# Norm boundaries of a two-layer diffusion trunk: affine step in halves, token tiles multiplied one by one, modulation blocks loaded from GpSimd's queue

## The reference, cut to what matters

```
h = rmsnorm(x, g_mix_pre) * (1 + scale1) + shift1
x = x + gate1 * rmsnorm(mixer(h), g_mix_post)
h = rmsnorm(x, g_ffn_pre) * (1 + scale2) + shift2
x = x + gate2 * rmsnorm(conv_ffn(h, ...), g_ffn_post)
```

## Time and profile before

| | us |
|---|---|
| median of 3 runs (1643.89 to 1649.33) | 1647.64 |
| the profiled execution | 1646.06 |
| its span in the trace | 1644.3 |
| PE busy | 1555.4 (95%) |
| DVE busy | 1087.6 (66%) |
| ACT busy | 700.5 (43%) |
| POOL busy | 117.2 (7%) |
| mean granted TensorE clock | 0.972 of full |

### The profile page before, as it was taken

How to read it: one execution, slowest core, us unless ns; L and a number is a source line. 1 busy time by engine, 2 the same in 40 slices (tenths; PEclk the granted TensorE clock), 3 DMA queues, 4 the chain that set the end, 5 groups by cost and what they waited for, 6 DMA issues and landing times.

```text
span 1644.3 us, 27983 instructions
## 1 busy us (share of the span) xinstructions
PE 1555.4 (95%) x10553; PEld 1414.5 (86%) x10553; DVE 1087.6 (66%) x2082; ACT 700.5 (43%) x1263; POOL 117.2 (7%) x128
## 2 busy tenths in 40 slices
PE   6799898989999999999989989989899999999997
PEld 2699687879998789998779988768799988999986
DVE  5598766888777867778884248872866641466544
ACT  6631666354443234443252237662644432344332
POOL 1250220000000000000010032410000000000000
PEclk8799899999999999999989989999999999999999
DMA  8234101613334763334642220102222222222222
GB/s 328 105 115 129 33 2 59 211 52 105 113 115 147 217 174 115 115 105 168 198 135 69 75 81 2 44 4 76 61 82 77 70 71 89 73 70 76 70 81 92
DMA packets 45953, 164.54 MB, mean 100 GB/s; under 512 B 5584, under 2 KB 6608, under 8 KB 45104
## 3 DMA queue, kind: packets, MB, share of 16 engines
q1 hardware_dynamic: 42336, 152.00, 28.5%
q0 software_dynamic: 2320, 10.54, 2.0%
q10 hardware_dynamic: 1216, 0.92, 0.2%
HBM read 159.87 MB, written 3.57 MB: 99 GB/s over the span
## 4 chain that ended last, share of the span: by engine, by line
PE 81%; DVE 7%; DMA 2%; issue 2%; ACT 1%; ACTq 0%; DVEq 0%; SPq 0%
PE ps L1842 22%; PE ps L1843 22%; PE ps L1943 13%; PE ps L1935 6%; PE ps L2100 4%; PE ps L2129 4%; PE ps L2042 3%; PE ps L2115 3%; DMA work<-in_wmodt 2%; DVE work L1081 1%; PE ps L1867 1%; PE ps L2034 1%; PE ps L2116 1%; PE ps L2134 1%; DVE product L1081 1%
## 5 line engine op out<-in xcount | busy, mean ns | idle before, releaser
L1842 PE MATMUL ps<-hh,whi 128*128 128x320 f32 x864 | 268.4, 311 | 7.7 <-DVE wlo L1067 3.8
L1842 PE MATMUL ps<-hh,wlo 128*128 128x320 f32 x864 | 267.7, 310 | 0.0
L1843 PE MATMUL ps<-hh,wlo 128*128 128x320 f32 x864 | 267.6, 310 | 0.0
L1842 PE MATMUL ps<-hl,whi 128*128 128x320 f32 x864 | 267.6, 310 | 0.0
L1843 PE MATMUL ps<-hl,whi 128*128 128x320 f32 x864 | 267.6, 310 | 0.0
L1843 PE MATMUL ps<-hh,whi 128*128 128x320 f32 x864 | 267.6, 310 | 0.0
L618 ACT ACTIVATE whi<-raw 128x1024 fp32r<-128x1024 f32 (+1 forms) x112 | 117.0, 1046 | 319.8 <-PE ps L1843 286.8
L612 ACT ACTIVATE whi<-raw 128x1024 fp32r<-128x1024 f32 (+1 forms) x70 | 72.1, 1033 | 264.3 <-PE ps L1943 173.6
L1943 PE MATMUL ps<-whi,ffh 128*128 128x512 f32 x440 | 171.9, 391 | 3.4 <-DVE wlo L1067 2.6
L1067 DVE TENSOR_TENSOR wlo<-raw,whi 128x1024 fp32r<-128x1024 f32 (+1 forms) x72 | 87.5, 1216 | 131.8 <-ACT whi L612 128.6
L1943 PE MATMUL ps<-wlo,ffh 128*128 128x512 f32 x440 | 171.3, 389 | 0.0
(11 more groups left out here) (226 smaller groups left out, 2897.8 us busy)
## 6 DMA issues: line engine op xcount, KB each, us to landing
raw<-in_w SPq DMA_DIRECT2D x174, 512.0 KB, 3.5
work<-in_wmodt SPq DMA_DIRECT2D x56, 512.0 KB, 3.6
ring<-in_wmodt SPq DMA_DIRECT2D x24, 512.0 KB, 4.3
work<-in_wmod SPq DMA_DIRECT2D x16, 512.0 KB, 6.8
grow<-gate_rows POOLq DMA_DIRECT2D x4, 1024.0 KB, 5.8
work<-in_rpb POOLq DMA_DIRECT2D x8, 448.0 KB, 4.5
x<-in_x SPq DMA_DIRECT2D x5, 512.0 KB, 7.9
out_x<-x SPq DMA_DIRECT2D x5, 512.0 KB, 2.6
```

Source lines behind the costliest of these rows:

```text
L1842: T.matmul(bankA[s], slot(w, s, k), h[:, k, 0:HT], start=st, stop=sp_)
L1843: last = T.matmul(bankB[s], slot(w, s, k), h[:, k, HT:NT], start=st, stop=sp_)
```

## The change

1. The affine step of a tile is split in two halves of four instructions with a wait and a count of their own. `SCALAR_AFFINES` and `VECTOR_AFFINES` say who does which half; `affine_done` waits for both. The halves of tiles 0, 1, 3 and 4 are shared between both engines; in `mix_boundary` ACT does both of tile 2, in `fout1_boundary` they are shared too.
2. The orders of both engines in both boundaries are rewritten.
3. `piece` multiplies one slot by one token tile: 24 matmuls of 128 columns. It waits for the low part of that tile and slot only. PE turns tiles 0, 1 and 2 and then alternates pieces and the remaining turns.
4. Blocks 24 to 79 are issued by POOL's queue, in order, each after its buffer's last block is summed. `spread_gate(1, 0, 3)` stands behind block 55. SP's queue no longer waits for them.

```diff
+SCALAR_AFFINES = {"mix": ((0, 1), (1, 0), (2, 0), (2, 1), (3, 1), (4, 0)),
+                  "fout1": ((0, 1), (1, 1), (1, 0), (2, 0), (3, 0), (4, 1))}
+VECTOR_AFFINES = {"mix": ((0, 0), (1, 1), (3, 0), (4, 1)),
+                  "fout1": ((0, 0), (2, 1), (3, 1), (4, 0))}
...
+        def affine_done(engine, b, t):
+            kind = NORMED[b][1]
+            for half in range(2):
+                if (t, half) in SCALAR_AFFINES[kind]:
+                    engine.wait_ge(s_afa, len(SCALAR_AFFINES[kind]) * b + SCALAR_AFFINES[kind].index((t, half)) + 1)
+                else:
+                    engine.wait_ge(s_afd, len(VECTOR_AFFINES[kind]) * b + VECTOR_AFFINES[kind].index((t, half)) + 1)
...  SP's queue
-                if u == 23:
-                    sp.wait_ge(s_tl, 5)
-                if u == 45:
-                    sp.wait_ge(s_ffl, FH + 1)
-                if u == 79:
-                    sp.wait_ge(s_ffl, 2 * FH + 1)
                 for m in LOAD_AFTER.get(u, ()):
-                    sp.wait_ge(s_mused, chunk_before(m) + 1)
-                    chunk_in(m, chunk_buffer(m), ring0 if m < 24 else ring1)
+                    if m < 24:
+                        sp.wait_ge(s_mused, chunk_before(m) + 1)
+                        chunk_in(m, chunk_buffer(m), ring0)
...  affine on ACT (on DVE alike)
-            def affine(b, t):
+            def affine(b, t, half):
-                if t == 2:
-                    act.wait_ge(s_tl, 5 * b + 1)
+                if t >= 2:
+                    act.wait_ge(s_tl, 5 * b + t - 1)
-                for k in range(KD):
+                for k in range(4 * half, 4 * half + 4):
...  mix_boundary on ACT, from square_x(b, 2) on, as it is now
                 square_x(b, 2)
+                deviation_x(b, 2)
+                hi(u)
+                affine(b, 0, 1)
+                hi(u + 1)
+                h_hi(b, 0)
+                affine(b, 1, 0)
+                square_x(b, 3)
                 square_y(b, 1, 4)
...  mix_boundary on DVE
                 update_x(b, 3)
+                inverse_x(b, 2)
                 norm_x(b, 1)
-                affine(b, 0)
+                affine(b, 0, 0)
+                affine(b, 1, 1)
+                norm_x(b, 2)
                 lo(u)
                 h_lo(b, 0)
-                inverse_x(b, 2)
                 lo(u + 1)
+                inverse_x(b, 3)
                 gate_mixed(b, 1, 4)
-                norm_x(b, 2)
-                inverse_x(b, 3)
                 norm_x(b, 3)
...  POOL
+            pool.wait_ge(s_tl, 5)
+            for m in range(24, 80):
+                pool.wait_ge(s_mused, chunk_before(m) + 1)
+                if m == 36:
+                    pool.wait_ge(s_ffl, FH + 1)
+                if m == 67:
+                    pool.wait_ge(s_ffl, 2 * FH + 1)
+                b = chunk_buffer(m)
+                pool.dma_start(ring1[b], a["wmodt"][m]).then_inc(s_mlate[b], 16)
+                if m == 55:
+                    pool.wait_ge(s_yf, 10)
+                    pool.wait_ge(s_coef, 8)
+                    spread_gate(1, 0, 3)
...  PE
-            def piece(u0, c0, c1, bank, f, start, final):
-
-                for s in range(2):
-                    for k in range(KD):
-                        for n, (w, h) in enumerate(((whi, hh), (whi, hl), (wlo, hh))):
-                            last = T.matmul(ps[:, 2 * s + bank, f:f + c1 - c0], slot(w, s, k), h[:, k, c0:c1], ...)
+            def piece(b, u0, s, t):
+                pe.wait_ge(s_lo, u0 + s + 1)
+                pe.wait_ge(s_tl, 5 * b + t + 1)
+                if t == 0 and s == 0:
+                    affine_done(pe, b, 1)
+                if t == 0 and s == 1:
+                    pe.wait_ge(s_yf, 10 * yi + 5 + 3)
+                if t == 2 and s == 1:
+                    pe.wait_ge(s_yf, 10 * yi + 10)
+                bank, f = (0, P * t) if t < 2 else (1, P * (t - 2))
+                for k in range(KD):
+                    for n, (w, h) in enumerate(((whi, hh), (whi, hl), (wlo, hh))):
+                        last = T.matmul(ps[:, 2 * s + bank, f:f + P], slot(w, s, k), h[:, k, tile(t)], ...)
+            def mix_boundary(b, u0):
+                turn(b, 0)
+                turn(b, 1)
+                turn(b, 2)
+                piece(b, u0, 0, 0)
+                piece(b, u0, 1, 0)
+                turn(b, 3)
+                piece(b, u0, 0, 1)
+                piece(b, u0, 1, 1)
+                piece(b, u0, 0, 2)
+                turn(b, 4)
+                piece(b, u0, 1, 2)
+                piece(b, u0, 0, 3)
+                piece(b, u0, 1, 3)
+                piece(b, u0, 0, 4)
+                piece(b, u0, 1, 4)
```

More of the change, by code:

```diff
@@ L151, in chunks_loaded, with late_chunks_loaded @@
     return early + sum(1 for i in range(12, m + 1) if chunk_buffer(i) == b)
+def late_chunks_loaded(m):
+    return sum(1 for i in range(24, m + 1) if chunk_buffer(i) == chunk_buffer(m))
 def chunk_before(m):
@@ L910, in mix_boundary @@
                 deviation_y(b, 4)
-                affine(b, 2)
+                affine(b, 2, 0)
+                affine(b, 2, 1)
                 h_hi(b, 2)
@@ L914, in mix_boundary @@
                 deviation_x(b, 4)
+                affine(b, 3, 1)
                 h_hi(b, 3)
+                affine(b, 4, 0)
                 h_hi(b, 4)
@@ L947, in fout1_boundary @@
                 deviation_x(b, 4)
+                affine(b, 3, 0)
                 h_hi(b, 3)
+                affine(b, 4, 1)
                 h_hi(b, 4)
@@ L1183, in affine @@
                 dve.wait_ge(s_tr, 5 * (b + 1) + t + 1)
+                if t >= 2:
+                    dve.wait_ge(s_tl, 5 * b + t - 1)
                 st = stream(t)
-                for k in range(KD):
+                for k in range(4 * half, 4 * half + 4):
                     last = V.tensor_scalar(hft[t % 2][:, k, :], turn_bank(t)[:, tile(k)],
@@ L1493, in mix_boundary @@
                 h_lo(b, 3)
-                affine(b, 4)
+                affine(b, 4, 1)
                 h_lo(b, 4)
@@ L2047, in boundary @@
-            def boundary(b, u0):
-                yi = TOKEN_PHASES.index(NORMED[b])
[L2050 to L2056, removed]
-                turn(b, 4)
[L2058 to L2062, removed]
+            def piece(b, u0, s, t):
+                yi = TOKEN_PHASES.index(NORMED[b])
+                pe.wait_ge(s_lo, u0 + s + 1)
[9 more added lines that the diff above has]
+                    for n, (w, h) in enumerate(((whi, hh), (whi, hl), (wlo, hh))):
+                        last = T.matmul(ps[:, 2 * s + bank, f:f + P], slot(w, s, k), h[:, k, tile(t)],
+                                        start=t in (0, 2) and k == 0 and n == 0, stop=t in (1, 4) and k == KD - 1 and n == 2)
+                if t == 4:
+                    last.then_inc(s_unit, 1)
@@ new lines, in fout1_boundary @@
+            def fout1_boundary(b, u0):
+                turn(b, 0)
+                turn(b, 1)
+                turn(b, 2)
+                piece(b, u0, 0, 0)
+                piece(b, u0, 1, 0)
+                piece(b, u0, 0, 1)
+                turn(b, 3)
+                piece(b, u0, 1, 1)
+                piece(b, u0, 0, 2)
+                turn(b, 4)
+                piece(b, u0, 1, 2)
+                piece(b, u0, 0, 3)
+                piece(b, u0, 1, 3)
+                piece(b, u0, 0, 4)
+                piece(b, u0, 1, 4)
@@ L2172, in ffn @@
                 down_units(layer, 1)
-            boundary(0, UNITS[(0, "fin0")][0])
+            mix_boundary(0, UNITS[(0, "fin0")][0])
             ffn(0)
@@ L2177, in _ @@
             fu1 = feature_unit((1, "in"))
-            boundary(1, u1)
+            fout1_boundary(1, u1)
             dense_pairs(u1 + 2, fu1 + 2, 5)
@@ L2188, in _ @@
             mix_units(1)
-            boundary(2, UNITS[(1, "fin0")][0])
+            mix_boundary(2, UNITS[(1, "fin0")][0])
             ffn(1)
```

95 lines of the change are left out of this document (41 added, 54 removed).

## The result

The changed kernel takes 1696.2 us (median of 4 runs, 1681.65 to 1726.43); the kernel before 1647.76 in the same comparison. Two of the four executions (1707.59 and 1726.43) were slow ones, at a lower mean granted clock (0.951 and 0.937 against 0.963 and 0.965), and the ratio, 1.022 (95% interval 1.0185 to 1.0253), is taken without them. Slower, as forecast, but far more: the two profiled executions took 1684.82 and 1646.06, +38.8 us, where the prediction had +15.2. Both the median and the profiled execution lie outside the forecast's range, 1650 to 1673.

What follows compares the result with a forecast made beforehand. PE bounds the kernel (81%), and the change aims at 25.3 us of its waits. Profiled 1646.06, +16.7 for the boundaries, -1.5 for the modulation blocks: 1661.3, predicted as 1661; range 1650 to 1673.

Steps and rivals of the forecast that it cites:

- What bounds the kernel: PE, 81% of it; its largest wait, 19.9 us for normed token tiles, lies nearly all in the three boundaries.
- Part 1, 112 ns a thin product: Boundary products become 240 matmuls of 128 columns at 112 ns, adding 10.0 us of PE work a boundary, 30 in all.
- Rival A: Boundaries: thin matmuls go by their columns, 66 ns at 128 columns; faster, 1629 us; chance 0.06.
- Part 2, the walk: New orders stepped through each boundary: first product about 7 us in; 36.0, 37.4 and 36.1 us, clock included.
- Part 2, the clock term: At each boundary, new idle spells of 2.3 to 2.9 us cost 0 to 2 us by low clock; 1 taken.
- Rival D: Boundaries: the low clock spreads over the thin matmuls, 4 us more in each, 1673 us; chance 0.07.
- Part 3: Modulation blocks on POOL's queue and the later gate rows' write: -1.5 us in sum, from -6 to +9.
- the gain at 592: PE's idle of 2.78 us at 592.60 and its low clock go when the gate rows' write moves: -4.5 us.
- the blocks' landing: Modulation blocks issued by POOL land +0.5 us later each than SP's 3.6 us, from -0.4 to +1.5.
- Rival C: Block queue: POOL's blocks land 1.5 us later, costing time in fout0 and fout1; 1672 us; chance 0.13.

Runs made afterwards that it cites:

- e2: The kernel before with each boundary product cut into matmuls of 128 columns, nothing else changed: 1689.7 us, ratio 1.0268.
- e4: The changed kernel with unread 256-column float32 matmuls in PE's idle spells of each boundary: 1662.6 us, ratio 1.0075 to the kernel before.
- e1: The changed kernel with PE's boundary order of before and wide products (256, 256 and 128 columns): 1643.54 us, ratio 0.9963 to the kernel before.
- e3: The kernel before with only modulation blocks 24 to 79 moved to GpSimd's queue and the gate spread behind block 55: 1643.51 us, ratio 0.9954.
- e8: The kernel before with boundary products cut to 128 columns and unread float32 matmuls filling PE's idle spells: 1674.6 us, ratio 1.0220.
- e11: The changed kernel with eight unread 256-column float32 matmuls in each boundary, behind the first 24 thin products: 1683.29 us, ratio 1.0221 to the kernel before.

## Why the prediction was wrong

- **What bounds the kernel**: right. The change went for PE's 19.9 us of waits, and 12 of them went.
- **Part 1, 112 ns a thin product**: right. There are 720 of them, and at full clock, as from 368.99 on, their step is 0.112 us; e2 grew by 9.6 and 9.2 us where the clock was the same. Rival A (66 ns, 1629 us) fell. The sustained pace of about 81 ns for 128 columns that the Trainium skill gives, page "TensorE: Matmul & The Clock Gate", section "Back-to-back issue gap", does not hold here: the trace has 112.
- **Part 2, the walk**: right. The first product came 6.8, 8.9 and 6.8 us after the boundary's start, and PE never waited after it; with the clock held (e4) the boundaries came to 35.6, 37.6 and 35.6 us against 36.0, 37.4 and 36.1.
- **Part 2, the clock term: this step failed.** "I take 1" a boundary, "between 0 and 2". The boundaries came out 5.3, 14.4 and 5.5 us above the forecast's 36.0, 37.4 and 36.1 (together 25). e4, which fills the idle and changes nothing else, is 5.8, 14.2 and 6.0 us shorter than the changed kernel (together 26): that is the clock's price, where the sum had 1 each. The term was read from stretches in which transposes and wide products followed the idle: there some 4 us at 1.2 GHz, and I carried that duration over to thin products. It is not a property of the idle. Counted from the end of the last idle spell, the clock came back after 3.0 to 4.9 us in all nine boundaries of before, e1 and e3, and after 3.5 and 3.1 us in e2's mix boundaries, where only transposes had run; in the changed kernel it took 12.1, 29.7 and 12.8 us, and 25.3 in e2's second boundary. At the low clock a thin product takes 0.213 us instead of 0.112: 12.1 us of them lose 5.7, and 29.7 lose 14.1, which is what was measured. A slip of reading beside it changes nothing: the 3.67 us of the 16 transposes is a record's length, and by starts they took 3.3 where 1.75 would do.
- **Rival D** was the mechanism, at 0.07 and with 4 us a boundary. My argument against it (the 128-column stretch to 370.82 held its pace) proved nothing: that stretch began when the clock had long been back, so it tells that thin products keep a high clock and not that they bring it back. e8 shows the one, e2's second boundary and e11 the other.
- **Part 3**: the gain at 592 came as forecast (the idle is gone, the gate write is at 605.35, 34 us later rather than 20), and the blocks' landing rose from 3.6 to 3.9 us, +0.3 for my +0.5. The stretch from the first to the second boundary gave -0.9 in the profiled run for -1.5. Rival C did not happen. No run showed GpSimd's issues held back by VectorE, which the Trainium skill's page "DMA: Bandwidth & Descriptors", section "SWDGE vs HWDGE vs iDMA", made possible.

Sum of the profiled run: forecast 1661.3, +25 in the boundaries, -2 elsewhere: 1684.8.

## What to carry to other kernels

When a change makes products narrower behind a wait, price the clock with narrow products and not from what followed the wait before (here transposes and wide products). If none is in the trace, put the whole narrow stretch at the lower level as the upper bound. Where a wait in front of narrow matmuls cannot be removed, unread wide matmuls in it can be worth far more than they cost (22 us here), but with wide products behind it they brought about 1 us a boundary and nothing that could be measured in the whole. And look at when small scattered DMAs run: the best gain of this case, 0.5%, was one wait that moved an 8 KB write out of a stretch full of loads.

## What the hardware showed unexpectedly

- The granted clock stayed at 0.50 for 30.7 us, for 29.7 of which PE was busy with 128-column products and 16 transposes, and returned some 4 us into 256-column float32 matmuls put among such products. The Trainium skill, page "TensorE: Matmul & The Clock Gate", section "What's actually happening", puts the penalty of the clock's ramp under 1% of a typical kernel's span. This trace does not agree: 26 us of boundaries between the changed kernel and e4 are 1.5% of the span.
- Transposes of 128 columns brought the clock back in 3.5 and 3.1 us (e2, mix boundaries), where 20 us of 128-column products with about the same step did not (e2, second boundary).
- A write of 8 KB element by element took 9 to 13 us, and four loads of 512 KB issued beside it some 12 us instead of 3.6.
